# A delta-rule projection whose activations are loaded in two halves between the weight pieces, its first block multiplied in parts, with filler matmuls ahead of it

## The reference

```python
proj = x @ w_in                                  # x: 256 x 1024, w_in: 1024 x 4112
qkv, z, b, a = jnp.split(proj, ...)              # 3072, 1024, 8, 8 columns
qkv = jax.nn.silu(causal_dwconv(qkv, conv_w))    # 4 taps
```

## Time and profile before

| | |
|---|---|
| time, median of 3 runs | 1590.62 us (1589.98 to 1591.07) |
| the profiled execution, its own time | 1593.2 us |
| its span, first to last instruction | 1591.3 us |
| mean granted TensorE clock | 0.982 |
| busy: TensorE, VectorE, ScalarE, GpSimd | 1508.8, 1019.4, 696.2, 34.8 us |
| DMA | 443.45 MB, mean 279 GB/s |

### The profile page before, as it was taken

How to read it: one execution, slowest core, us unless ns; L and a number is a source line. 1 busy time by engine, 2 the same in 40 slices (tenths; PEclk the granted TensorE clock), 3 DMA queues, 4 the chain that set the end, 5 groups by cost and what they waited for, 6 DMA issues and landing times.

```text
span 1591.3 us, 24618 instructions
## 1 busy us (share of the span) xinstructions
PE 1508.8 (95%) x10552; PEld 1132.9 (71%) x10552; DVE 1019.4 (64%) x1446; ACT 696.2 (44%) x915; POOL 34.8 (2%) x34
## 2 busy tenths in 40 slices
PE   7999898999998999999999998999999999999986
PEld 7988778888997888888888887986434434443435
DVE  5776778999869688889888987785121121212127
ACT  5673335454443467667677675353101101110114
POOL 0000100000020000000000001000000000000001
PEclk9999999999999989999999999999999999999998
DMA  8431044344631449889989897378999999999981
GB/s 342 159 148 56 2 157 182 133 159 159 242 117 58 183 175 363 332 329 351 352 336 336 325 367 302 126 314 361 426 427 428 428 428 428 428 427 427 428 366 40
DMA packets 37841, 443.45 MB, mean 279 GB/s; under 512 B 5600, under 2 KB 6112, under 8 KB 10464
## 3 DMA queue, kind: packets, MB, share of 16 engines
q1 hardware_dynamic: 36576, 438.35, 68.9%
q10 hardware_dynamic: 1152, 3.46, 0.6%
HBM read 440.75 MB, written 1.05 MB: 278 GB/s over the span
## 4 chain that ended last, share of the span: by engine, by line
PE 75%; DVE 13%; DMA 7%; ACT 2%; issue 2%; SPq 0%; PEldq 0%; PEld 0%; ACTq 0%; DVEq 0%
PE psum L232 73%; DMA sb_spare<-moe_up 3%; DVE sb_ring_r L1304 2%; DMA sb_ring<-moe_wide 1%; DMA sb_ring<-ffn_wide 1%; DVE sb_split L2027 1%; DVE sb_work L2738 1%; DMA sb_lnp<-ln_rows 1%; PE psum L2534 1%; PE psum L2082 1%; DMA sb_work<-b_im 0%; DVE sb_work L1334 0%; DVE sb_ring_r L509 0%; DVE sb_work L1333 0%; DVE sb_work L1332 0%
## 5 line engine op out<-in xcount | busy, mean ns | idle before, releaser
L2027 DVE TENSOR_TENSOR sb_split<-sb_ring,sb_split 128x2048 fp32r<-128x2048 f32 (+1 forms) x144 | 301.1, 2110 | 44.8 <-ACT sb_split L2021 43.8
L232 PE MATMUL psum<-sb_work 64*64 64x64 f32 (+11 forms) x3392 | 285.9, 335 | 19.0 <-DVE sb_work L2738 7.8
L2021 ACT ACTIVATE sb_split<-sb_ring 128x2048 fp32r<-128x2048 f32 (+1 forms) x144 | 253.2, 1773 | 89.2 <-PE psum L232 60.6
L232 PE MATMUL psum<-sb_split 128*128 128x512 f32 (+1 forms) x912 | 268.7, 384 | 0.2 <-DVE sb_split L2341 0.2
L232 PEld LDWEIGHTS psum<-sb_work 128*64 128x64 f32 (+4 forms) x3392 | 148.6, 143 | 140.7 <-issue 119.5
L232 PE MATMUL psum<-sb_split,sb_lnp_r 128*128 128x512 f32 (+1 forms) x768 | 230.4, 374 | 1.4 <-DVE sb_split L2310 1.4
L232 PEld LDWEIGHTS psum<-sb_split 128*128 128x128 f32 x912 | 169.9, 188 | 30.7 <-DVE sb_split L2341 0.7
L232 PEld LDWEIGHTS psum<-sb_split,sb_lnp_r 128*128 128x128 f32 x768 | 142.7, 188 | 21.8 <-DVE sb_split L2310 1.6
L232 PE MATMUL psum<-sb_xT_r,sb_ring_r 128*128 128x256 f32 x512 | 144.3, 283 | 0.0
L2736 DVE TENSOR_TENSOR sb_work<-sb_work,psum 128x512 f32<-128x512 f32 x16 | 11.0, 689 | 169.4 <-ACT sb_work L2648 169.4
L2648 ACT ACTIVATE sb_work<-psum 128x512 f32<-128x512 f32 x16 | 9.6, 597 | 238.7 <-PE psum L232 238.7
(11 more groups left out here) (468 smaller groups left out, 2677.7 us busy)
## 6 DMA issues: line engine op xcount, KB each, us to landing
sb_ring<-moe_wide SPq DMA_DIRECT2D x48, 2048.0 KB, 8.8
sb_work<-moe_up SPq DMA_DIRECT2D x33, 2048.0 KB, 25.2
sb_ring<-w_dense SPq DMA_DIRECT2D x23, 2048.0 KB, 8.5
sb_ring<-moe_last SPq DMA_DIRECT2D x24, 1536.0 KB, 8.3
sb_ring<-moe_up SPq DMA_DIRECT2D x18, 2048.0 KB, 25.1
sb_work<-moe_down SPq DMA_DIRECT2D x17, 2048.0 KB, 24.4
sb_ring<-ffn_wide SPq DMA_DIRECT2D x12, 2048.0 KB, 7.8
sb_ring<-moe_down SPq DMA_DIRECT2D x9, 2048.0 KB, 25.5
```

Source lines behind the costliest of these rows:

```text
L232: return nc.tensor.matmul(o, lhsT, rhs, start=start, stop=stop, **kw)
L2021: act.activation(wh[half_home(e, i)][:, 0:half_size(i)], half_raw(e, i), ACT.Copy).then_inc(sem("m1_high"), 1)
L2027: v.tensor_tensor(wl[home][:, 0:half_size(i)], half_raw(e, i), wh[home][:, 0:half_size(i)].bitcast(F32), ALU.subtract).then_inc(sem("m1_sp ...
```

## The change

Six edits go together.

- `x_cols` is loaded as two halves of four chunks (512 KB each). SyncE issues half 0, piece 0, half 1, piece 1, piece 2, piece 3. Each half has a semaphore of its own.
- ScalarE rounds half 0, piece 0, half 1, piece 1, piece 2; VectorE takes the remainders in the same order. `conv_w` has another semaphore and is awaited only behind piece 2.
- Block 0 is multiplied in parts: for each half the four high x high products, which need the high parts alone, and then the eight others, which need the low parts.
- GpSimd first sets `warm`, 128 unused columns of `DT`, to zero, and TensorE multiplies them with themselves twenty times into bank 5 before anything else.
- The counts of `gdn_high`, `gdn_low` and `zg_done` are one higher from there on (`gd_at`, `WO`, 4 for 3).
- Two semaphores are shared with loads that come much later (`conv_mix2_loaded`, `x1_p_loaded`), with the later waits raised by 16.

```diff
+        def gd_at(s):
+            return 2 if s == 0 else 2 + s + 1
         def gd_low(v, s):
-            v.wait_ge(sem("gdn_high"), 1 + s + 1)
+            v.wait_ge(sem("gdn_high"), gd_at(s))
...
-        WO = 1 + GD_PIECES
+        WO = 2 + GD_PIECES
...
         def gd_split(pe, s):
-            pe.wait_ge(sem("gdn_low"), 1 + s + 1)
+            pe.wait_ge(sem("gdn_low"), gd_at(s))
...
+        warm = DT.rearrange("p i c -> p (i c)")[:, 3 * P:4 * P]
...
         def gdn_tensor(pe):
-            for c in range(QKV):
+            pe.wait_ge(sem("zg_done"), 1)
+            for _ in range(20):
+                mm(bank[5][:, 0:P], warm, warm)
+            wh_, wl_, o = gd_buffer(0), gd_piece(ring_r, 0), bank[0][:, 0:SEQ]
+            for i in range(2):
+                pe.wait_ge(sem("gdn_high"), 2 + i)
+                for k in range(4 * i, 4 * i + 4):
+                    mm(o, wh_[:, k, :], gxh[:, k, :], k == 0, False, skip_group_check=True)
+                pe.wait_ge(sem("gdn_low"), 2 + i)
+                for k in range(4 * i, 4 * i + 4):
+                    mm(o, wl_[:, k, :], gxh[:, k, :], False, False, skip_group_check=True)
+                    ins = mm(o, wh_[:, k, :], gxl[:, k, :], False, k == DC - 1, skip_group_check=True)
+            ins.then_inc(sem("qkv_ps"), 1)
+            for c in range(1, QKV):
...
         def gdn_scalar(act):
-            act.dma_start(conv_w, I["conv_w"]).then_inc(sem("first_loaded"), 16)
-            act.wait_ge(sem("first_loaded"), 32)
-            act.activation(gxh[:, :, :], xT[:, :, :], ACT.Copy).then_inc(sem("gdn_high"), 1)
-            for s in range(3):
-                gd_high(act, s)
+            act.dma_start(conv_w, I["conv_w"]).then_inc(sem("conv_mix2_loaded"), 16)
+            for i in range(2):
+                act.wait_ge(sem(("x0_loaded", "x1_p_loaded")[i]), 16)
+                act.activation(gxh[:, 4 * i:4 * i + 4, :], xT[:, 4 * i:4 * i + 4, :], ACT.Copy).then_inc(sem("gdn_high"), 1)
+                gd_high(act, i)
+            gd_high(act, 2)
+            act.wait_ge(sem("conv_mix2_loaded"), 16)
...
         def gdn_vector(v):
-            v.wait_ge(sem("gdn_high"), 1)
-            v.tensor_tensor(gxl[:, :, :], xT[:, :, :], gxh[:, :, :].bitcast(F32), ALU.subtract).then_inc(sem("gdn_low"), 1)
-            for s in range(3):
-                gd_low(v, s)
+            for i in range(2):
+                o = slice(4 * i, 4 * i + 4)
+                v.wait_ge(sem("gdn_high"), 2 * i + 1)
+                v.tensor_tensor(gxl[:, o, :], xT[:, o, :], gxh[:, o, :].bitcast(F32), ALU.subtract).then_inc(sem("gdn_low"), 1)
+                gd_low(v, i)
+            gd_low(v, 2)
...
         def gdn_gpsimd(g):
+            g.memset(warm, 0.0).then_inc(sem("zg_done"), 1)
...
-            sp.dma_start(xT[:, :, :], I["x_cols"]).then_inc(sem("first_loaded"), 16)
...
             for i in range(4):
+                if i < 2:
+                    sp.dma_start(xT[:, 4 * i:4 * i + 4, :], I["x_cols"][:, 4 * i:4 * i + 4, :])\
+                      .then_inc(sem(("x0_loaded", "x1_p_loaded")[i]), 16)
                 sp.dma_start(ring[:, 0, i * D:(i + 1) * D], I["w_dense"][DENSE_AT[U_QKV]][:, i * D:(i + 1) * D])\
                   .then_inc(sem(f"piece_loaded{i}" if i < 3 else "unit_loaded0"), 16)
```

More of the change, by code:

```diff
@@ L557, in head_sums @@
             if r == 0:
-                pe.wait_ge(sem("zg_done"), 3)
+                pe.wait_ge(sem("zg_done"), 4)
             for i in range(4):
@@ L1029, in gated @@
                 dve_link(v, v.tensor_tensor(of[:, h, :], of[:, h, :], rq_s[:, h, :], ALU.mult))
-                v.wait_ge(sem("zg_done"), 3 + h + 1)
+                v.wait_ge(sem("zg_done"), 4 + h + 1)
                 for e in range(HEADS):
@@ L3035, in mix2_loads @@
             for name, dst in (("wsT", wsT), ("g_sgu", g_sgu)):
-                act.dma_start(dst, I[name]).then_inc(sem("mix2_loaded"), 16)
+                act.dma_start(dst, I[name]).then_inc(sem("conv_mix2_loaded"), 16)
         def mix2_scalar(act):
@@ L3080, in mix2_vector @@
             v.memset(zT[:, :, 0:CONV2_TAPS - 1], 0.0)
-            v.wait_ge(sem("mix2_loaded"), 32)
+            v.wait_ge(sem("conv_mix2_loaded"), 16 + 32)
             v.tensor_tensor(wsT[:, :, :], wsT[:, :, :], bc(upto_t, 1, SGU_HEADS), ALU.mult).then_inc(sem("mix2_operand"), 1)
@@ L3173, in emb_tensor @@
         def emb_tensor(pe, j, h):
-            pe.wait_ge(sem("p_loaded"), 32)
+            pe.wait_ge(sem("x1_p_loaded"), 16 + 32)
             for k in range(2):
@@ L3423, in _ @@
                 sp.wait_ge(sem("dense_used"), D_WOUT2)
-                sp.dma_start(w_ple, I["w_ple"].rearrange("p (k n) -> p k n", k=2)).then_inc(sem("p_loaded"), 16)
-                sp.dma_start(pT, I["pT"]).then_inc(sem("p_loaded"), 16)
+                sp.dma_start(w_ple, I["w_ple"].rearrange("p (k n) -> p k n", k=2)).then_inc(sem("x1_p_loaded"), 16)
+                sp.dma_start(pT, I["pT"]).then_inc(sem("x1_p_loaded"), 16)
                 released(M2_RING[6])
```

## The result

| kernel | median, us | lowest to highest | runs | span of the profiled run | its mean granted clock |
|---|---|---|---|---|---|
| before | 1590.70 | 1589.24 to 1591.60 | 6 | 1591.3 | 0.982 |
| changed | 1598.49 | 1595.15 to 1603.60 | 6 | 1596.0 | 0.978 |

The ratio is 1.0052, with an interval of 1.0035 to 1.0068: the change made the kernel 7.8 us slower. The forecast was 1586.3 us, faster, with 0.04 on slower. It was wrong, sign and all.

The account below looks back on a forecast made before the run. It took TensorE, waiting 11.5 us for its first operands and then unbroken, as the bound; 3.3 (earlier dense work) + 0.47 (matmuls already done) + 0.5 (clock) = 4.3 us gave 1586.3 us, range 1584.6 to 1588.7.

Parts of the forecast that it names:

- The fillers: Ahead of block 0: twenty f32 matmuls take 4.3 us, may raise the clock, and are credited with 0.5 us.
- They delay nothing: Ahead of block 0: the twenty matmuls end at 5.3 to 5.5 us, before the first operand at 7.0.
- the first part: Opening on what bounds the kernel: TensorE idles 11.5 us, then every block waits for TensorE alone.
- An earlier end of the first blocks is passed on one for one: First projection: time gained in its first blocks carries through fully, unless something fed from outside binds.
- My rival for slower: Blocks 0 to 8: the broken first block keeps the clock at 1.2 GHz; 25 us of it gives 1595; chance 0.04.
- dense work: TensorE in block 0: uninterrupted matmuls start at 8.2 us instead of 11.5, 3.3 us earlier.
- The first load: Head of the load queue: x half 0 lands at 4.4 us, 1.3 us before the whole load's 5.73.
- a high clock from block 0 on: First projection: no slow stretch, then unit 1 binds; gain 5.5 us, 1585.1; chance 0.16.
- a warm-up that is mostly lost: Blocks 0 and 1: a slow stretch remains, a little shorter, worth 0.5 us; main forecast, chance 0.60.
- the forecast's 2.8 us: TensorE between the fillers and dense matmuls, 5.4 to 8.2 us: a gap with only 0.5 to 0.9 us of work.
- the rival's working: Block 4: unit 1's first high starts at 16.2 us, the bank frees at 19.9 against 19.5, stall 0.4 us.
- The upper branch: Ahead of block 0: fillers at 0.43 us each end at 9.6 us, and the gain is 2 us less.

Follow-up runs that it names:

- e1: The changed kernel again with no edit, timed beside the kernel before: 1596.87 us, ratio 1.0046.
- e4: The changed kernel with its gate products spread in four parts behind blocks 8 to 11, twenty fillers kept: 1593.91 us, 1.0030 times the kernel before.
- e11: The changed kernel with five fillers of 128x512 instead of twenty of 128x128: 1590.06 us, 0.9992 times the kernel before.
- e12: The changed kernel with five fillers of 128x512 and the gate products spread behind blocks 8 to 11: 1589.56 us, 0.9985 times the kernel before.
- e7: The changed kernel with ten fillers of 128x128 instead of twenty: 1590.79 us, 1.0017 times the kernel before.
- e3: The changed kernel without the twenty fillers, loads in halves and block 0 in parts kept: 1589.13 us, 0.9986 times the kernel before.
- e8: The changed kernel without fillers and with the gate products spread behind blocks 8 to 11: 1587.81 us, 0.9983 times the kernel before.
- e6: The kernel before with only twenty fillers of 128x1 and their memset added: 1598.30 us, 1.0046 times the kernel before.
- e9: The kernel before with only twenty small fillers (32x32 weights, one column) added: 1596.63 us, 1.0028 times the kernel before.
- e2: The kernel before with only the memset and twenty fillers of 128x128 added: 1597.18 us, 1.0041 times the kernel before.

## Why the prediction was wrong

**The step that failed.** It is the sentence in "The fillers": "They delay nothing", with the one in the first part on which it leans, "An earlier end of the first blocks is passed on one for one, unless something fed from outside binds in its place." I asked of the fillers what they delay (nothing), what they do to the clock (a gain), and left out that they are 80 more records in a stream that is itself fed from outside. What the runs showed in its place: fillers alone on the kernel before cost 1.0041, 1.0046 and 1.0028, the last with 2.3 us of work, and the new start without them 0.9986. The loss comes from the number of instructions ahead of the rest, not from their work, and it doesn't grow with that number: +256 gave 1.0008. That much is shown: seven results with twenty fillers lie from 1.0028 to 1.0052, and each interval is above 1; six with none, five, ten or sixty-four lie from 0.9983 to 1.0017, and each interval holds 1. That TensorE waits for its code at places that move with the number of records ahead is shown by the count of 256 and by the packets. It accounts for some 1.5 us; for the rest the mechanism is open.

**My rival for slower** (a long stretch at 1.2 GHz in blocks 0 to 8) had the wrong place: the blocks ran at the higher level from 9.0 us, and in that profile all of the loss lies behind 88 us. Its chance, 0.04, counted only that one way of losing.

**What held of the start.** The steps came in the order of the forecast, each later than it. Measured (forecast): x half 0 read at 5.39 (4.4), high of piece 0 from 6.65 (6.0), `gxh` half 1 from 7.93 (7.5), low of piece 0 over at 8.97 (8.2), dense work from 9.03 (8.2). The halves come 1.3 us apart as the landing gap of the earlier trace rows said. The first load was sized wrongly: I gave half a load 1.3 us less than the whole one, and it was read only 0.34 us before the 5.73 at which the whole one had landed. So dense work began 2.5 us earlier than before (9.03 against 11.50), not 3.3; the rest of the 5.27 us at block 0 comes from the four high products that were done by then and from the clock.

**The clock.** I gave 0.16 to a high clock from block 0 on and 0.60 to a warm-up that is mostly lost. The first happened, in the changed kernel, e1, e4, e11 and e12. It was partly luck in length: the fillers lasted until 7.59, not 5.4, so that no break like the forecast's 2.8 us followed them. In e7 one did (2.84 us), and the warm-up was lost as the forecast had it. The 5.5 us of that rival were reached (5.45 at block 1), then block 4 waited until 21.80, against 19.9 in the rival's working, since unit 1's first piece was split at 18.25, not at 16.2. The fillers were worth 1.18 us at block 0 (the changed kernel against e3), by a high clock in place of a slow stretch, and nothing at block 8, where e3 is 0.74 us ahead. Five wide ones kept theirs: 11.75 at block 0 and 34.64 at block 8.

**The fillers' length.** 6.61 us, from 0.98 to 7.59, where I took 4.3. The row counts x18 in 3.8 us, and I read 18 products; they are 18 records, two to a product. The upper branch (0.43 us each) was right for the first 3.9 us, until the clock rose, and 0.22 held from there. It cost little, since the first operand was ready only at 7.7.

**The gate products.** I named them as a reader of the small loads and not as a place where the clock can go. The fall at them took 2.8 us (9.21 against 6.40) of the 3.75 us lead in the changed kernel. It isn't a fixed price: it is in six of eleven profiles, at 2.8 us in one and 1.5 in five, and in none of the three with spread gates (e4, e8, e12). Those gain 2.5, 0.5 and 1.1 us over their like by the ratios, together in the right direction and singly within the intervals.

**What stays open.** Why a start that is 4 to 5 us earlier gives only 2.2 to 2.7 us by the ratios in e3, e8 and e12, whose intervals hold 1; the lower clock may take some of it in e8 and e12. Why the new start and the fillers bring the mean clock down, and whether the moved breaks do. Why unit 1 lands 1.1 to 1.7 us later with twenty fillers of 128 columns.

## What to carry to other kernels

Instructions in an idle hole of an engine aren't free when thousands follow them: they shift where the engine must wait for its code, and this kernel lost 4.5 to 8 us by twenty of them, only partly in such waits. Before crediting such an edit, put the same number of nearly empty instructions in the same place and time that alone; and if work is wanted there, take few wide instructions rather than many narrow ones. And a lead of 4 us at the start of a kernel of 1,590 is not yet a gain of 4 us at its end: follow it in the trace to where it is spent, here 2.8 us at one group of 16 short products.

## What the runs showed of the hardware

- An f32 product stands in the records as two weight loads and two matmuls (20 products, 40 and 40), and takes 0.43 us with 128 columns at the slower pace and 0.22 us at the faster one; 20 took 6.61 us, at both.
- At the slower pace one column is no shorter than 128 with 128x128 weights: both have 0.213 us from record to record. Twenty products of one column took 8.69 us, all at that pace (e6), and 2.29 us with 32x32 weights (e9).
- Fillers of 128 columns came to the faster pace after 3 to 5 us (changed, e1, e2, e4, e7). After an idle 2.8 us (e7) or 4.2 us (e2) the next matmuls were at the slower one again.
- After 6.6 or 7.5 us of fillers and gaps of less than 0.6 us the first dense block ran at 118 ns a matmul. At 32 short records in a row the granted clock fell to 0.50 in six of eleven profiles, for 3 us or more, and stayed at 1.00 in the five others.
- TensorE's waits for code stand 256 records apart, or a multiple of it, and end 1.2 to 1.6 us after a 16 KB packet has landed (80 waits in 14 traces). The longest, 3.1 to 5.0 us, stand behind a branch.
- Half of a load of 1 MB at the head of its queue came only 0.34 us earlier than the whole; the following 512 KB loads came 1.3 us apart.
- The kernel before scatters by 1.4% from end to end over 103 runs (1579.25 to 1601.09), and its time follows its mean granted clock, 1.19 us for 0.001.
